# Four dense tiles of a hybrid attention and experts block, split over the halves of their contraction, with the first six weight pieces in another order

## The reference

```python
mod = (silu(c) @ w_ada + b_ada)                      # 6 x 1024 numbers
sh1, sc1, gt1, sh2, sc2, gt2 = split(mod, 6)
h = rmsnorm(x, norm1_g) * (1.0 + sc1) + sh1          # 256 x 1024
proj = h @ w_in                                      # 13 projections
qa, ka, va, qi, ki, wi, qb, kb, vb, gb, lr, ga, gbm = split(proj)
# ya: attention over 64 keys that an indexer (qi, ki, wi) selects; yb: gated linear attention (qb, kb, vb, lr)
# x = x + gt1 * ((sigmoid(ga) * (ya @ w_a) + sigmoid(gbm) * (yb @ w_b)) @ w_out)
# x = x + gt2 * moe(rmsnorm(x) * (1 + sc2) + sh2)    # 32 experts, 4 for each token
```

## Time and profile before

| | us |
|---|---|
| three runs | 1467.7, 1471.64, 1471.86 |
| median | 1471.64 |
| the profiled execution | 1467.8 |
| its span, first to last instruction | 1466.0 |
| PE busy | 1378.1 |
| VectorE busy | 498.9 |
| ScalarE busy | 249.7 |
| mean rate of the transfers | 330 GB/s |

### The profile page before, as it was taken

One profiled execution on the slowest core, in us unless ns is written; L12 is line 12 of the kernel. 1 busy time (PEld: TensorE's weight loads), 2 busy tenths in 40 slices (PEclk: granted clock), 3 DMA queues, 4 the chain that ended last, 5 costly groups with the idle time before them and its releaser, 6 DMA issues.

```text
span 1466.0 us, 17062 instructions
## 1 busy us (share of the span) xinstructions
PE 1378.1 (94%) x6275; PEld 619.7 (42%) x6276; DVE 498.9 (34%) x1032; ACT 249.7 (17%) x426; POOL 10.7 (1%) x35
## 2 busy tenths in 40 slices
PE   6999999999989999999999999999999999899996
PEld 3888455888443333333333333333333333223321
DVE  2250024556543233333333333323323323232233
ACT  3311025100011111111111111111111111111111
POOL 0000000000000000000000000000000000000000
PEclk9999999999969999999999999999999999999998
DMA  9734433899437639999699999979999999999994
GB/s 351 252 137 141 146 118 128 270 348 341 183 153 291 259 132 413 418 417 416 250 416 418 419 418 416 414 307 419 418 418 417 416 419 418 418 416 418 418 419 201
DMA packets 113088, 483.38 MB, mean 330 GB/s; under 512 B 10102, under 2 KB 10266, under 8 KB 80202
## 3 DMA queue, kind: packets, MB, share of 16 engines
q1 hardware_dynamic: 111666, 477.95, 81.9%
q0 software_dynamic: 1056, 4.06, 0.9%
q10 hardware_dynamic: 344, 1.07, 0.2%
HBM read 482.00 MB, written 1.05 MB: 329 GB/s over the span
## 4 chain that ended last, share of the span: by engine, by line
PE 73%; DMA 12%; SPq 9%; ACT 4%; issue 1%; DVE 1%; DVEq 0%; ACTq 0%
PE bank L1411 24%; PE bank L1100 14%; PE bank L1440 13%; DMA gu_slot<-in_w_gate_up 10%; PE bank L1109 8%; SPq L345 4%; SPq L350 4%; PE bank L1358 4%; PE bank L1390 3%; PE bank L1367 1%; ACT gx L633 1%; ACT xg L635 1%; ACT actT L637 1%; DMA piece<-in_w_ada 1%; DMA piece<-in_w_in 1%
## 5 line engine op out<-in xcount | busy, mean ns | idle before, releaser
L1411 PE MATMUL bank<-gu_slot,xg 128*64 128x512 f32 x2304 | 518.3, 597 | 18.6 <-DMA gu_slot<-in_w_gate_up 16.1
L1411 PEld LDWEIGHTS bank<-gu_slot,xg 128*64 128x64 f32 x2304 | 159.3, 137 | 365.8 <-issue 312.7
L1440 PE MATMUL bank<-dn_slot,actT 128*64 128x512 f32 x1152 | 255.1, 595 | 24.7 <-ACT actT L637 24.7
L1020 DVE TENSOR_TENSOR rowt<-bank,gt 128x512 f32<-128x512 f32 x144 | 92.8, 686 | 389.0 <-PE bank L1390 387.8
L1100 PE MATMUL bank<-hT,piece 128*128 128x256 f32 x704 | 155.2, 382 | 0.2 <-DMA piece<-in_w_in 0.2
L1440 PEld LDWEIGHTS bank<-dn_slot,actT 128*64 128x64 f32 x1152 | 79.4, 137 | 177.3 <-issue 144.0
L1100 PEld LDWEIGHTS bank<-hT,piece 128*128 128x128 f32 x704 | 134.5, 192 | 20.1 <-issue 1.1
L631 ACT ACTIVATE sig<-gcl 128x512 f32<-128x512 f32 x36 | 22.7, 630 | 571.4 <-DVE gcl L1038 571.4
L1038 DVE TENSOR_SCALAR gcl<-bank 128x512 f32<-128x512 f32 x36 | 24.9, 691 | 272.6 <-PE bank L1411 272.6
L1024 DVE TENSOR_TENSOR xs<-xs,rowt 128x512 f32<-128x512 f32 x144 | 93.1, 688 | 2.5
L1109 PE MATMUL bank<-piece,hT 128*128 128x512 f32 x192 | 83.2, 593 | 0.0
(11 more groups left out here) (279 smaller groups left out, 781.8 us busy)
## 6 DMA issues: line engine op xcount, KB each, us to landing
gu_slot<-in_w_gate_up SPq DMA_DIRECT2D x256, 1024.0 KB, 17.2
dn_slot<-in_w_down SPq DMA_DIRECT2D x128, 1024.0 KB, 17.2
piece<-in_w_in SPq DMA_DIRECT2D x17, 2048.0 KB, 8.8
piece<-in_w_ada SPq DMA_DIRECT2D x12, 2048.0 KB, 12.8
piece<-in_w_branch_a SPq DMA_DIRECT2D x2, 2048.0 KB, 8.5
piece<-in_w_branch_b SPq DMA_DIRECT2D x2, 2048.0 KB, 8.7
piece<-in_w_out SPq DMA_DIRECT2D x2, 2048.0 KB, 8.6
xs<-in_x ACTq DMA_DIRECT2D x1, 1024.0 KB, 8.9
```

The costliest lines, as they stand in the source:

```text
L1020: ins = V.tensor_tensor(rowt[:, t, :], sum_bank[t][q][:], gt2[:, cols_], ALU.mult)
L1411: ins = M(bank[u][64 * q:64 * q + 64, :], xg[:, k % 4, 64 * (k // 4):64 * (k // 4) + 64], gu_slot[k][:, cols_], start=(k == 0), stop=(k == ...
L1440: ins = M(bank[5][64 * q:64 * q + 64, :], actT[:, f % 4, 64 * (f // 4):64 * (f // 4) + 64], dn_slot[f // 2][:, f % 2, 512 * q:512 * q + 51 ...
```

## The change

Four things change together. The first six pieces come in the order ada0, ada2, qi, qa, ada1, ada3, and the short transfers move two places back in `PIECES`. colA now holds the lower halves of sh1 and sc1, colB the upper ones, with one function, `columns_ready`, for both. The upper half of x (xT1, xT3) is copied unscaled into `hT` by ScalarE, and VectorE scales it there, k by k, after colB. And the four tiles qi0, qi1, qa0 and qa1 are begun on k 0 to 3 and finished later on k 4 to 7 by `half_feature`; since two groups of columns of one bank stay open meanwhile, one matmul on zeros opens the whole bank.

```diff
 PLAN = (
-    [("ada0", "A"), ("ada1", "A"), ("xT0", "V"), ("xT1", "A"), ("xT2", "V"), ("xT3", "V"), ("ada2", "A")]
+    [("ada0", "A"), ("ada2", "A"), ("xT0", "V"), ("xT2", "V"), ("xT1", "A"), ("xT3", "A"), ("colA", "V")]
...
 PIECES = (
-    [("ada", i, f"ada{i}") for i in range(4)]
+    [("ada", 0, "ada0"), ("ada", 2, "ada2"), ("qi", 0, "qi1"), ("qa", 0, "qa1"), ("ada", 1, "ada1"), ("ada", 3, "ada3")]
...
@@ sync
-                if n == 3:
+                if n == 5:
                     sp.dma_start(wsm[:, :, 0:96], columns(w_in, col["ki"], 96)).then_inc(wsm_in, 16)
                     sp.dma_start(wsm[:, :, 96:P], columns(w_in, col["lr"], 32)).then_inc(wsm_in, 16)
-                if n == 4:
+                if n == 6:
                     sp.dma_start(wgl[:], w_gate_lr[0]).then_inc(wgl_in, 16)
...
@@ scalar
-            for i in range(4):
+            for i in (0, 2):
                 take(f"ada{i}", (modp[i][:], tile(f"ada{i}")[:], ACT.Copy, {}))
-            act.wait_ge(gain1_ready, 1)
-            take("xT1", *[(hT[:, k, 0:P], tile("xT1")[:, (k % 4) * P:(k % 4 + 1) * P], ACT.Identity,
-                           dict(scale=gain1[:, k:k + 1], bias=shift1[:, k:k + 1])) for k in range(4, 8)])
+            for t in range(TT):
+                take(f"xT{2 * t + 1}", (hT[:, 4:8, t * P:(t + 1) * P], tile(f"xT{2 * t + 1}")[:].rearrange("p (k t) -> p k t", k=4),
+                                        ACT.Copy, {}))
+            for i in (1, 3):
+                take(f"ada{i}", (modp[i][:], tile(f"ada{i}")[:], ACT.Copy, {}))
...
@@ vector
+            def columns_ready(name, k0):
+
+                ks = slice(k0, k0 + 4)
+                wait_tile(dve, name)
+                step(V.tensor_tensor(shift1[:, ks], tile(name)[:, 0:4], bcol[:, ks], ALU.add))
+                chain(V.tensor_tensor(gain1[:, ks], tile(name)[:, 4:8], bcol[:, KT + k0:KT + k0 + 4], ALU.add), out_dve)
+                chain(V.tensor_tensor(gain1[:, ks], gain1[:, ks], g1[:, ks], ALU.mult))
+
+            columns_ready("colA", 0)
...
             take_xT(0)
             take_xT(2)
-            wait_tile(dve, "colB")
-            chain(V.tensor_tensor(gain1[:, 4:8], tile("colB")[:, 0:4], bcol[:, KT + 4:2 * KT], ALU.add), out_dve)
-            chain(V.tensor_tensor(gain1[:, 4:8], gain1[:, 4:8], g1[:, 4:8], ALU.mult), gain1_ready)
-            take_xT(3)
+            columns_ready("colB", 4)
+            wait_out(dve, "xT3")
+            for k in range(4, KT):
+                step(V.tensor_scalar(hT[:, k, :], hT[:, k, :], gain1[:, k:k + 1], shift1[:, k:k + 1], ALU.mult, ALU.add), high_ready)
...
@@ tensor
+            def half_feature(kind, c, high):
+
+                w = arrived(kind, c)
+                zero = nought[:].bitcast(BF16)
+                for j in range(2):
+                    if not high:
+                        ps = begin(f"{kind}{2 * c + j}")
+                        M(ps[:], zero[:, 0:P], zero, start=True, stop=False)
+                    ps = tile(f"{kind}{2 * c + j}")
+                    for f in range(2):
+                        a = (2 * j + f) * P
+                        for k in range(4 * high, 4 * high + 4):
+                            if high and j == 0 and f == 0:
+                                pe.wait_ge(high_ready, k - 3)
+                            ins = M(ps[:, f * T:(f + 1) * T], w[:, k, a:a + P], hT[:, k, :], start=False, stop=(f == 1 and k == KT - 1))
+                    if high:
+                        full(ins)
+
             modulation_part("ada0", 0)
...
+            ps = begin("colA")
+            modulation_columns(ps, 0, 0)
+            full(modulation_columns(ps, 4, 2))
+            wait_out(pe, "xT2")
+            pe.wait_ge(nought_ready, 1)
+            half_feature("qi", 0, False)
+            half_feature("qa", 0, False)
             modulation_part("ada1", 1)
...
             modulation_part("ada3", 3)
...
+            half_feature("qi", 0, True)
             pe.wait_ge(wsm_in, 32)
...
-            by_feature("qi", 0, hT)
+            half_feature("qa", 0, True)
             wait_out(pe, "small")
...
-            by_feature("qa", 0, hT)
```

More of the change, by code:

```diff
@@ L30 @@
 PLAN = (
-    [("ada0", "A"), ("ada1", "A"), ("xT0", "V"), ("xT1", "A"), ("xT2", "V"), ("xT3", "V"), ("ada2", "A")]
-    + [("colA", "V"), ("ada3", "A"), ("colB", "V")]
-    + [("small", "A"), ("qi0", "A"), ("qi1", "A"), ("wi", "A"), ("z0", "A"), ("z1", "A"), ("qa0", "A"), ("qa1", "A")]
[3 rows of a table added]
     + [("sx0", "A"), ("sx1", "A")] + [(f"sy{i}", "A") for i in range(4)] + [("qa2", "A"), ("qa3", "A")]
@@ L50 @@
 TAKER = dict(PLAN)
-FIRST = ["ada0", "ada1", "ada2", "colA", "xT0", "xT2", "ada3", "colB", "xT1", "xT3"]
-TAKEN = [(name, TAKER[name]) for name in FIRST] + PLAN[10:]
+FULL = (["ada0", "ada2", "xT0", "xT2", "xT1", "xT3", "colA", "ada1", "ada3", "colB"]
+        + ["qi0", "qi1", "small", "qa0", "qa1", "wi", "z0", "z1"] + [name for name, _ in PLAN[18:]])
+FULL_COUNT = {name: n + 1 for n, name in enumerate(FULL)}
+FIRST = ["ada0", "ada2", "colA", "xT0", "xT2", "xT1", "xT3", "ada1", "ada3", "colB", "qi0", "qi1", "small", "qa0", "qa1"]
+TAKEN = [(name, TAKER[name]) for name in FIRST] + PLAN[15:]
 OUT_COUNT = {name: 1 + sum(1 for _, w in TAKEN[:n] if w == who) for n, (name, who) in enumerate(TAKEN)}
 PIECES = (
-    [("ada", i, f"ada{i}") for i in range(4)]
-    + [("qi", 0, "qi1"), ("qa", 0, "qa1"), ("qa", 1, "qa3"), ("qb", 0, "qb1"), ("kb", 0, "kb1"), ("ka", 0, "ka1"),
[2 rows of a table added]
        ("ka", 1, "ka3"), ("vb", 0, "vb1"), ("vb", 1, "vb3"), ("va", 0, "va1"), ("va", 1, "va3"), ("gb", 0, "gb1"),
@@ L221, in hybrid_block @@
         eofw = sb("eofw", 177, [MAXB + 1, 3 * E])
+        nought = small("nought", [1, 256])
         first_slot = small("first_slot", [P, TT])
@@ L470, in _, with take_qk @@
             step(A(root[:, 0:TT], sqe[:, 0:TT], ACT.Sqrt), xroot_ready)
-            for i in range(4):
+            for i in (0, 2):
                 take(f"ada{i}", (modp[i][:], tile(f"ada{i}")[:], ACT.Copy, {}))
-            act.wait_ge(gain1_ready, 1)
-            take("xT1", *[(hT[:, k, 0:P], tile("xT1")[:, (k % 4) * P:(k % 4 + 1) * P], ACT.Identity,
-                           dict(scale=gain1[:, k:k + 1], bias=shift1[:, k:k + 1])) for k in range(4, 8)])
+            for t in range(TT):
[3 more added lines that the diff above has]
+                take(f"ada{i}", (modp[i][:], tile(f"ada{i}")[:], ACT.Copy, {}))
+            def take_qk(dst, kind, i):
+                take(f"{kind}{i}", (dst[:, 2 * i:2 * i + 2, :].rearrange("p a b -> p (a b)"), tile(f"{kind}{i}")[:], ACT.Copy, {}))
+            for i in range(2):
+                take(f"qi{i}", (qiT[:, 2 * i:2 * i + 2, :].rearrange("p a b -> p (a b)"), tile(f"qi{i}")[:], ACT.Copy,
+                                dict(scale=IDX_DIM ** -0.5)))
             take("small", (kiT[0:64, :], tile("small")[0:64, 0:T], ACT.Copy, {}),
@@ L481, in _ @@
                  (lrT[:], tile("small")[96:96 + RANK, 0:T], ACT.Copy, {}))
-            for i in range(2):
-                take(f"qi{i}", (qiT[:, 2 * i:2 * i + 2, :].rearrange("p a b -> p (a b)"), tile(f"qi{i}")[:], ACT.Copy,
-                                dict(scale=IDX_DIM ** -0.5)))
+            take_qk(qaT, "qa", 0)
+            take_qk(qaT, "qa", 1)
             take("wi", (wis[:].rearrange("p t h -> p (t h)"), tile("wi")[:, 0:TT * IH], ACT.Copy, {}))
@@ L495, in _ @@
             step(A(softp[:], softp[:], ACT.Ln, bias=1.0), softp_ready)
-            def take_qk(dst, kind, i):
-                take(f"{kind}{i}", (dst[:, 2 * i:2 * i + 2, :].rearrange("p a b -> p (a b)"), tile(f"{kind}{i}")[:], ACT.Copy, {}))
             def take_rows(dst, kind, i):
@@ L1129, in modulation_columns @@
                 return ins
-            modulation_part("ada0", 0)
-            modulation_part("ada1", 1)
[L1133 to L1141, removed]
+            def half_feature(kind, c, high):
[14 more added lines that the diff above has]
+                        full(ins)
+            modulation_part("ada0", 0)
+            for t in range(TT):
+                if t == 0:
+                    modulation_part("ada2", 2)
+                pe.wait_ge(xn_ready, t + 1)
+                transposes(f"xT{2 * t}", xn, t, 0)
+            for t in range(TT):
+                transposes(f"xT{2 * t + 1}", xn, t, 1)
+            ps = begin("colA")
[5 more added lines that the diff above has]
+            half_feature("qa", 0, False)
+            modulation_part("ada1", 1)
             modulation_part("ada3", 3)
-            full(modulation_columns(begin("colB"), 0, 3))
+            ps = begin("colB")
+            modulation_columns(ps, 0, 1)
+            full(modulation_columns(ps, 4, 3))
+            half_feature("qi", 0, True)
             pe.wait_ge(wsm_in, 32)
```

17 lines of the change are left out of this document (4 added, 13 removed), and 3 rows, old and new, of tables (PIECES, PLAN).

## The result

| | median us | lowest to highest | runs |
|---|---|---|---|
| before | 1468.26 | 1466.4 to 1471.86 | 14 |
| after | 1473.96 | 1470.58 to 1476.94 | 14 |

A forecast was written before the change was run, and what follows sets the result against it. PE was taken to bound the start, with 1.1 us of reachable idle time. Full-clock cost 2.1 us plus 3.2 for two low-clock stretches gave 5.3 us, on a base of 1469.75: 1475.1 us, range 1469 to 1479.4.

The forecast's parts named there:

- (a): Columns and stall before the low halves, 23.7 to 28.85 us: expected to cost one low-clock stretch, 1.6 us.
- What bounds the start: Up to the dense tiles PE bounds, not transfers; pieces arrive early, and the shift there persists to the expert stage.
- The stall before the low halves: PE waits for VectorE's last hT instruction (xT2) with nothing else to do: 3.25 us, to 28.85.
- The one before the high half: After colB, PE waits for VectorE before the high half of qi: 0.95 us, to 50.5.
- The opening matmuls: Four bf16 matmuls on zeros opening the banks of the low halves: 0.9 us, bounds 0.44 and 1.5.
- The first matmuls up to colA: Until 23.71 us nothing moves; a first low half before 28 us would show the forecast wrong.
- The clock: Low-clock stretches in thin PE work before the dense tiles: two at 1.6 us each, 3.2 us together.
- (b): Columns and stall before the high half of qi, 47.6 to 50.5 us: left out, no fall expected.
- (c): wi, z and the index products on 64 rows, 5.2 us long: one low-clock stretch expected, 1.6 us.
- rival 2: All three thin stretches before the dense tiles fall to low clock: 6.9 us slower, 1476.6; chance 0.17.
- Rival 4: At the start, before's long runs come from qi landing 4 us late, which the change saves; faster side, chance 0.07.
- ScalarE's and VectorE's moved work: Gate work between z and the score tiles: scoring near 82.5, selection ends near 104, costing PE nothing; cover some 20 us.

The follow-up runs named there:

- e1: The changed kernel with three unused f32 matmuls of 512 columns in the stall before the first low half; 1469.31 us, ratio to before 1.0014.
- e10: The changed kernel with unused matmuls in both stalls and without the opening matmuls on zeros, start and column order unchanged; 1469.14 us, ratio to before 0.9999.
- e3: The changed kernel with wi and z placed between the two tiles of qa's high half; 1474.88 us, ratio to before 1.0052.
- e5: The changed kernel without the four opening matmuls on zeros, only a bank's first matmul carrying the start flag; ratio to before 1.0009.
- e4: The kernel before with modulation parts ordered ada0, ada2, ada1, ada3, columns by halves, VectorE scaling the upper half, qi and qa whole and last; ratio 0.9994.
- e8: The kernel before with only the six unused matmuls at the start added; ratio to before 1.0007.
- e6: The changed kernel with colA's columns ahead of the transposes of xT1 and xT3; 1471.26 us, ratio to before 1.0017.
- e9: The changed kernel with columns early, no opening matmuls and unused matmuls at the start, but none in the two stalls; ratio to before 1.0000.
- e7: The changed kernel with columns early, no opening matmuls, and unused matmuls in both stalls and at the start; 1465.44 us, ratio to before 0.9974.

## Why the prediction was right, and where it was not

It gave 1475.1 us in a range of 1469 to 1479.4 and 5.3 us over before; 1473.96 us and 5.3 us by the ratio were measured. The middle of 1469.75 that I took for before was 1.5 us too high; 14 runs give 1468.26. The mechanism is the forecast one in its main part, two new waits for VectorE and a fall at (a); that the 5.3 us are met so closely is luck, since several terms were off by 1 to 2 us in both directions. By its steps:

- **What bounds the start**: right. All weights were early; after the second modulation piece PE waited for no transfer up to the dense tiles. The 7.29 us at 78 us stand unchanged at 412 us.
- **The stall before the low halves**: 3.25 us predicted, 3.27 measured. **The one before the high half**: 0.95, measured 1.06.
- **The opening matmuls**: 0.9 us, bounds 0.44 and 1.5; measured 0.53 for the first, in low clock, and 0.31 for each other, 1.46 in all. And the dense groups between them stretched: e1 against e10 makes the four worth 1.9 us at full clock. The term was too small by 1.0, and its upper bound of 1.5 too low; such a matmul doesn't run at the 0.22 of a dense record that I took.
- **The first matmuls up to colA**: I had "nothing moves", and a first low half before 28 us as a sign of being wrong. It was opened at 26.90. In the profiled execution ada2 took 3.22 us and the transposes 1.97 instead of 3.14, so colA's columns began 1.9 us earlier than the 23.64 at which before went on. In e3, e5 and e10 ada2 took 3.64 as in before, but the transposes 2.1 to 2.2, and in all six profiles of split kernels without `warm_up` that have the transposes ahead of the columns these began between 21.79 and 22.66 us, and the low halves were opened before 28. With one such trace of before it is open whether its 3.14 us are the rule there. Either way this worked against the loss: before, which waits for its pieces (e4, e8), could not have used it.
- **The clock**: 3.2 us predicted for two stretches at 1.6. (a) was the right place, but its price was too low: over the full-clock time of the low halves it cost 2.8 us in after, 1.6 in e3, 1.7 in e5, 2.4 in e6 and 2.9 in e9. The row that I priced it with lasted 3.3 us at 0.50. Here the low stretch lasted 6.8 us in after, e6 and e9, where it began in the stall, and 3.4 in e3 and e5, where it began with the low halves. (b), which I left out, fell in five of nine split kernels at 1.4 to 1.7 us; (c), which I counted as sure, fell in one of eight. So two of its clock terms were exchanged. The profiled execution has all three, the prediction's rival 2, and its 7.29 us are near that rival's 6.9; what the median execution of after has no trace shows.
- **The sum for the profiled execution**, by the distances between PE's starts: 3.27 + 1.06 + 1.86 for stalls and opening matmuls, 3.03 + 1.68 + 1.66 for the three falls (the first with 0.22 for the first opening matmul), less before's idle time 1.12, its own fall 1.69, the earlier columns 1.85, small's 0.52 and 0.08 for parts and columns: 7.3 us, against 7.29. The prediction's 3.96 us for small "with its stall" was misread: 1.97 + 1.99 are without it.
- **Rival 4, long executions of before by a late qi**: not borne out, as far as the runs tell. In the rounds of e9 and e10 six of 22 runs of before took 1471.3 to 1473 us, at a mean granted clock of 0.981 to 0.984, the others 0.984 to 0.987. Split kernels, which have every piece early, have such runs too (e1; e9 once, 1473.34 us at 0.981). So they go with the clock; none has a trace.
- **ScalarE's and VectorE's moved work**: right. Scoring began at 85.60 and the selection ended at 107.2 (82.5 and 104 predicted at full clock, which the falls move by some 3), VectorE had caught up at kb0, where it waits for PE, and PE noticed nothing. VectorE's instructions in order of time:

```profile
80.66 1.23 DVE L716 SCALAR_TENSOR_TENSOR z<-z,softp 128x1024 f32<-128x1024 f32 x1 [27.47 <-ACT softp L509]
...
107.22 1.29 DVE L759 SCALAR_TENSOR_TENSOR qe<-bank,qe 128x512 f32<-128x512 f32 x2
113.25 0.69 DVE L764 TENSOR_TENSOR kd<-bank,softp 128x512 f32<-128x512 f32 x1 [4.74 <-PE bank L1113]
```

- **The rule of the Trainium skill** ("TensorE: Matmul & The Clock Gate", "Why this matters for your kernels") that an idle gap between bursts puts the clock back: after, e3 and e5 agree at (a), with a gap of 3.27 us and a fall, and e1, with 0.58 and none. But e6 and e9 fell with a gap of 2.34 us, and the kernel before fell behind z with none, so a gap alone doesn't tell here where the clock falls. What share the work ahead of the gap has no run separates.

Where the hoped-for gain went: the split begins qi at 27 us instead of 36, but PE had nearly no idle time up to there to be filled (1.1 us). What was moved forward only moved the modulation parts and small back.

## What to carry to other kernels

Before splitting a product to start it early, count the idle time of the engine in the stretch that is to be filled, not the time in which the chain of waits names a transfer. A split has its own waits (here two for VectorE, 4.3 us), and each of them behind thin PE work can cost as much again through the clock (here 2.8 and 1.7 us); unused dense matmuls in the stall are a cheap way to see that, and to avoid it. And a start at full clock helps only where the transfers aren't the bound: on the kernel before it gave nothing, on the split one it brought the low halves forward and was one part of the 0.26%. Four small matmuls that only open a bank cost 1.9 us here, more than their own time.

## What the runs showed of the hardware

- A bf16 matmul of 512 columns on a one-row weight between dense f32 matmuls takes 0.31 us from its start to the next start (after), and four of them lengthen a stretch of 64 dense records by 1.9 us (15.87 us in e1, 14.01 in e10).
- In a bank in which one matmul carried the start flag, a second group of columns that begins without the flag gives a right result, without a matmul on zeros that opens the bank (e5, e7, e9, e10).
- Six unused f32 matmuls, three of them between the first two modulation parts, brought both parts from 3.64 to 1.92 us (e7, e8, e9).
- The clock can fall without any idle time, and it fell with a filler of 1.1 us in the stall (e10). A low stretch lasted 6.8 us where it began in a stall (after, e6, e9) and 3.4 where it began with dense work (e3, e5).
